# Two parts of one edit: the order of work behind the experts, and a norm's token factor behind its products

## What is computed

```python
# end of the first block
x = x + g2 * moe_ffn(h2, ...)          # each token: sum over 4 experts of weight * row, plus bias
x = rmsnorm(x, final_norm_w)
# the second block
h = concatenate([meta, x])             # 16 + 512 tokens
proj = rmsnorm_2(h, norm1_g) @ w_in    # queries first
...
h = h + mix @ w_out
hn = rmsnorm_2(h, norm2_g)             # h * rsqrt(mean(h*h) + eps) * g
gu = hn @ w_ffn_in                     # 1024 -> 2 * 2816
g, u = gu[..., :D_FF_2], gu[..., D_FF_2:]
h = h + (silu(g) * u) @ w_ffn_out
```

## Time and profile before

| | us |
|---|---|
| median of 3 runs | 3364.83 (3363.39 to 3370.04) |
| the profiled execution, its own time | 3360.08 |
| its span (first to last instruction) | 3358.2 |
| TensorE busy | 3205.9 (95%) |
| VectorE busy | 1330.0 (40%) |
| ScalarE busy | 725.3 (22%) |
| GpSimd busy | 400.2 (12%) |
| TensorE's share of the chain that ended last | 80% |
| VectorE's busy tenths in the slices of `ffn_in` | 2 to 4, mostly 3 |

### The profile page before, as it was taken

The page is one execution under the profiler, slowest core; times in us unless marked ns, Lnnn a source line. Parts: engine busy times, 40 slices in busy tenths (PEclk is TensorE's granted clock), DMA queues, the critical chain, the costliest instruction groups (busy, mean ns, idle before and its releaser), DMA issues.

```text
span 3358.2 us, 40420 instructions
## 1 busy us (share of the span) xinstructions
PE 3205.9 (95%) x13876; PEld 1897.5 (57%) x13877; DVE 1330.0 (40%) x2096; ACT 725.3 (22%) x1293; POOL 400.2 (12%) x312
## 2 busy tenths in 40 slices
PE   7999999999999999999999999999899999999999
PEld 5555555556488743333333333333587888788887
DVE  2544545455434532122122121221567577443342
ACT  3212121212021111111111111111224355211100
POOL 0222212132100100000000000000301254000000
PEclk9999999999999999999999999999899999999999
DMA  4211212124622369999999998888312121222111
GB/s 201 64 69 52 79 48 83 41 96 167 219 76 76 134 257 373 379 396 391 382 391 385 394 389 315 322 331 314 143 51 104 41 85 48 85 76 88 63 76 53
DMA packets 185079, 615.70 MB, mean 183 GB/s; under 512 B 18177, under 2 KB 55169, under 8 KB 174241
## 3 DMA queue, kind: packets, MB, share of 16 engines
q1 hardware_dynamic: 161216, 552.79, 43.1%
q0 software_dynamic: 10944, 39.85, 3.3%
q10 hardware_dynamic: 12832, 21.88, 1.8%
HBM read 578.01 MB, written 36.44 MB: 183 GB/s over the span
## 4 chain that ended last, share of the span: by engine, by line
PE 80%; DMA 5%; issue 5%; DVE 4%; POOL 2%; ACT 2%; SPq 1%; ACTq 0%; DVEq 0%; POOLq 0%
PE ps L322 24%; PE ps L2244 16%; PE ps L2218 11%; PE ps L1926 6%; PE ps L271 6%; DMA slot<-in_w_exp 5%; PE ps L1995 3%; PE ps L2467 2%; PE ps L2005 1%; PE ps L1971 1%; PE ps L1863 1%; PE ps L2439 1%; PE ps L2213 1%; PE ps L2422 1%; PE ps L2010 1%
## 5 line engine op out<-in xcount | busy, mean ns | idle before, releaser
L2244 PE MATMUL ps<-slot,xT_blk 128*64 128x512 f32 x3200 | 734.1, 599 | 26.4 <-DMA slot<-in_w_exp 23.8
L2244 PEld LDWEIGHTS ps<-slot,xT_blk 128*64 128x64 f32 x3200 | 218.0, 137 | 463.1 <-issue 376.1
L2218 PE MATMUL ps<-slot,aT 128*64 128x512 f32 x1632 | 361.1, 595 | 0.9 <-ACT aT L1634 0.9
L1926 PE MATMUL ps<-hT,slot 128*128 128x512 f32 (+1 forms) x896 | 308.9, 503 | 1.1 <-ACT small L1431 1.1
L2218 PEld LDWEIGHTS ps<-slot,aT 128*64 128x64 f32 x1632 | 116.9, 137 | 237.2 <-issue 237.2
L1926 PEld LDWEIGHTS ps<-hT,slot 128*128 128x128 f32 x896 | 168.9, 191 | 130.1 <-issue 121.1
L2966 DVE TENSOR_TENSOR gate<-ps,b_row 128x512 f32<-128x512 f32 x50 | 34.6, 692 | 517.8 <-PE ps L2244 517.6
L2587 DVE SCALAR_TENSOR_TENSOR conv<-ps,g_conv,conv 128x510 f32<-128x510 f32 (+1 forms) x224 | 133.3, 631 | 198.0 <-ACT conv L1444 194.6
L2962 DVE MEMSET b_there<- 128x1 f32 x50 | 3.0, 59 | 385.0 <-DMA b_few<-in_b_gu 376.4
L322 PE MATMUL ps<-in_t,in_s 128*128 128x264 f32 x528 | 124.8, 386 | 0.5 <-issue 0.5
L3334 POOL TENSOR_TENSOR token_there<-cst 128x1 f32<-128x1 f32 x25 | 4.9, 194 | 949.7 <-PE ps L2209 949.7
(11 more groups left out here) (501 smaller groups left out, 4769.8 us busy)
## 6 DMA issues: line engine op xcount, KB each, us to landing
slot<-in_w_exp SPq DMA_DIRECT2D x768, 512.0 KB, 8.5
in_w<-in_w_ffn SPq DMA_DIRECT2D x22, 1024.0 KB, 4.8
expert_rows<-zero SPq DMA_DIRECT2D x4, 4608.0 KB, 22.6
slot<-in_w_xbc SPq DMA_DIRECT2D x8, 2048.0 KB, 9.9
w_modT<-in_w_modT POOLq DMA_DIRECT2D x32, 512.0 KB, 3.5
rnn_w<-in_w_rnn SPq DMA_DIRECT2D x16, 1024.0 KB, 4.8
expert_rows<-y_row ACTq DMA_DIRECT2D x102, 128.0 KB, 5.6
out_w<-in_w_ffn_out SPq DMA_DIRECT2D x8, 1408.0 KB, 8.8
```

The lines of the kernel that those rows point to most:

```text
L1926: last = pe.matmul(ps[:, 2 * (m % 2) + part, 0:n], w[:, (k * 4 + m % 4) * P:(k * 4 + m % 4 + 1) * P], hT[:, k, c0:c0 + n], start=(k == 0), ...
L2218: last = pe.matmul(ps[h * UNIT:(h + 1) * UNIT, 6, :], aT[:, t, d * UNIT:(d + 1) * UNIT], slot[4 + d][:, t * D + h * 512:t * D + (h + 1) * ...
L2244: last = pe.matmul(ps[h * UNIT:(h + 1) * UNIT, 2 * s + t, :], xT_blk[:, k, s * UNIT:(s + 1) * UNIT], slot[i // 4][:, at:at + 512], start=( ...
```

## The change

Behind the experts:
- The filler ahead is 10 products instead of 19. `turn_sum` is split into `turn_last` (pick 3) and `turn_sum` (the identity over VectorE's sum). TensorE starts with block 0; the meta sum comes behind `turn_last(1)` and goes to bank 7. Each block's square sum moves to right behind the next block's turning.
- VectorE does picks 0, block 0 and picks 1 ahead of the meta steps; `invert(0)` and `invert(1)` come behind `add_picks(3)`, `add_back(2)` ahead of it.
- ScalarE takes a one-column square root ahead of the first pick, so that its table is there; the meta root comes behind the first block's square.
- GpSimd's `acc` waits for VectorE's last scaling (`scaled3_7`) instead of for the last square.

Second feed-forward:
- `Norm` is not used. ScalarE scales each tile of `h2nd` by the norm's weight straight into `xnT` and squares it; VectorE adds the squares tile by tile between the evictions of w_out; TensorE sums the result with 4 products, behind p1 and p2 of tile 0.
- The factor 1/root is multiplied on VectorE onto the four results of each tile (`by_root`: gate0, gate1, up0, up1), 88 multiplications of 128x264.
- The weight sums of tile 0 and `t1` are made between evictions; `in_s` and `in_t` change places in memory, and `root_m` moves.

```diff
-        keep_warm(19, 7)
-        back_act.after(pe, "meta_square")
-        for k in range(KD):
-            last = pe.matmul(ps[:, 6, 0:N_META], ones, square_meta[:, k, :], start=(k == 0), stop=(k == KD - 1))
-        back_pe.done(last, "meta")
+        keep_warm(10, 7)
...
+        turn_last(0)
         turn_sum(0)
+        turn_last(1)
+        back_act.after(pe, "meta_square")
+        for k in range(KD):
+            last = pe.matmul(ps[:, 7, 0:N_META], ones, square_meta[:, k, :], start=(k == 0), stop=(k == KD - 1))
+        back_pe.done(last, "meta")
         turn_sum(1)
         sum_squares(0)
+        turn_last(2)
         turn_sum(2)
+        sum_squares(1)
+        turn_last(3)
         turn_sum(3)
-        sum_squares(1)
         sum_squares(2)
         sum_squares(3)
```

```diff
+        back_dve.after(dve, f"bias{KD - 1}")
+        add_picks(0)
+        add_back(0)
+        add_picks(1)
         back_act.after(dve, "meta_root")
...
-        back_dve.after(dve, f"bias{KD - 1}")
-        add_picks(0)
-        add_back(0)
-        add_picks(1)
         add_picks(2)
         add_back(1)
+        add_back(2)
+        add_picks(3)
         invert(0)
-        add_picks(3)
-        add_back(2)
+        invert(1)
         add_back(3)
-        invert(1)
         invert(2)
```

```diff
+        act.activation(inverse_meta[:, 0:1], eps_col, ACT.Sqrt)
         first_pick(0)
+        first_pick(1)
+        squared(0)
         back_pe.after(act, "meta")
...
         first_pick(2)
-        squared(0)
         weighed(0)
         rooted(0)
         first_pick(3)
         squared(1)
         weighed(1)
+        rooted(1)
...
-        back_act.after(pool, f"square{TT - 1}")
+        back_dve.after(pool, f"scaled3_{KD - 1}")
```

```diff
-        norm2_2.on_act(act)
+        for j in range(KD):
+            out2.ev.after(act, f"tile{j}")
+            row2_act.done(act.activation(xnT[:, j, :], h2nd[:, j, :], ACT.Copy,
+                                         scale=prm[:, PRM["norm2_2"].start + j:PRM["norm2_2"].start + j + 1]), f"weighed{j}")
+            if j >= 3:
+                row2_dve.after(act, f"add{j - 2}")
+            row2_act.done(act.activation((square_m[j % 2] if j else square_sum)[:], h2nd[:, j, :], ACT.Square), f"square{j}")
...
-        norm2_2.on_pe(pe)
+        row2_act.after(pe, f"weighed{KD2 - 1}")
+        ffn_in.p1(pe, 0, in_ready(0))
         out2.ev.all(pe)
-        norm2_2.dve.after(pe, f"scaled{KD2 - 1}")
-        ffn_in.p1(pe, 0, in_ready(0))
-        norm2_2.dve.all(pe)
+        row2_act.after(pe, f"weighed{KD - 1}")
         ffn_in.p2(pe, 0)
+        row2_dve.after(pe, f"add{KD - 2}")
+        row2_act.after(pe, f"square{KD - 1}")
+        for l in range(2):
+            cols = slice(l * H2, (l + 1) * H2)
+            pe.matmul(ps[:, 5 + l, 0:H2], ones, square_sum[:, cols], start=True, stop=False)
+            last = pe.matmul(ps[:, 5 + l, 0:H2], ones, square_m[(KD - 1) % 2][:, cols], start=False, stop=True)
+        row2_pe.done(last, "sum")
         ffn_in.p1(pe, 1, in_ready(1))
```

```diff
+        def by_root(name, i, t, l):
+            ffn_in.dve.done(dve.tensor_tensor(t, t, root_m[:, l * H2:(l + 1) * H2], ALU.mult), f"{name}_{i}")
...
         in_done11(0)
+        for l in range(2):
+            cols = root_m[:, l * H2:(l + 1) * H2]
+            row2_act.after(dve, f"root{l}")
+            row2_dve.done(dve.reciprocal(cols, cols), f"inverse{l}")
+        row2_dve.all(dve)
+        ffn_in.dve.after(dve, "done11_0")
+        by_root("gate0", 0, ffn_gate[0][:, 0, :], 0)
```

More of the change, by code:

```diff
@@ L1209, in program @@
     out2 = Dense("out2", io["w_out2"], [0, 1], 1, 4, KD, H_PARTS, lambda k, p: attnT[:, k, p * H2:(p + 1) * H2], k_m(KD, 4), **second)
[L1210 to L1212 removed]
+    row2_act = Steps(sem("row2_act"), [n for j in range(KD) for n in (f"weighed{j}", f"square{j}")] + ["root0", "root1"])
+    row2_dve = Steps(sem("row2_dve"), [f"add{j}" for j in range(1, KD - 1)] + ["inverse0", "inverse1"])
+    row2_pe = Steps(sem("row2_pe"), ["sum"])
     FFN = KF
@@ L1832, in _ @@
         in_first11(0)
-        ffn_in.dve.after(act, "done11_0")
+        row2_pe.after(act, "sum")
+        for l in range(2):
+            row2_act.done(act.activation(root_m[:, l * H2:(l + 1) * H2], ps[:, 5 + l, 0:H2], ACT.Sqrt, scale=1.0 / D, bias=eps_col), f"root{l}")
+        ffn_in.dve.after(act, "gate0_0")
         ffn_in.act.done(in_silu(0, 0), "silu0_0")
```

109 lines of the change are left out of this document (62 added, 47 removed).

## The result

| | before | changed |
|---|---|---|
| median in the first comparison | 3364.11 us (4 runs, 3360.78 to 3370.04) | 3343.13 us (4 runs, 3338.86 to 3345.11) |
| ratio, 95% interval | | 0.9934 [0.9922, 0.9947] |
| median in a second comparison, in the last batch of runs | 3365.72 us (9 runs, 3361.99 to 3370.42) | 3339.39 us (4 runs, 3336.16 to 3342.15) |
| ratio, 95% interval | | 0.9915 [0.9900, 0.9930] |
| the profiled execution, its own time and span | 3360.08, 3358.2 us | 3344.28, 3342.5 us |

The changed kernel is faster by 21.0 us in one comparison and by 26.3 in the other, where 27.9 were forecast.

What follows compares the result with a forecast made beforehand. TensorE was taken to bound most of the span. 12.9 us after the experts plus 15.4 at the feed-forward less 0.45 gave 27.9 us; from 3360.08 to 3332.2, plus 4.75 to the median: 3337.0 us, range 3332 to 3346.

Steps and rivals of the forecast that it cites:

- What bounds the kernel, and the two places: Whole kernel: TensorE bounds most of the span; gains lie in the stage after the experts and the second feed-forward.
- Part two, 15.4 us: Entry of the second feed-forward: p7 of tile 0 starts at 2931.7 against 2947.12, 15.4 us earlier.
- tie: Feed-forward entry: ScalarE's silu and two copies end at 2931.6, level with TensorE; lateness 0 to 1.5 us, taken as 0.
- The loop, and +0.45 at its end: Second feed-forward's loop: four factor products per tile cost nothing inside it and 0.45 us at its end, up to 1.5.
- 3.2 us of room, 0.45 used: Feed-forward loop: the next weight sum is done 3.2 us before its p5; the fourth factor product uses 0.45.
- Adding back block 3 untouched by GpSimd (0 of 4.7): Stage after the experts: two GpSimd scalings over VectorE's adding back cost between 0 and 4.7 us, taken as 0.
- Block 2's scaling at 1.2: Stage after the experts: VectorE's scaling of block 2 takes 1.2 us without GpSimd beside it, seen at 2.60 before.
- GpSimd's additions behind the last scaling, 1.7 us: End of that stage: eight scalings at 0.34 us, so the first query tile takes 7.1 us instead of 8.8.
- The first query product 11.2 us earlier: Stage after the experts: the new order starts the query projection at 2413.5 instead of 2424.74.
- the first rival: Stage after the experts: low clock or late rows take part one's gain, 8 us lost, total 3345; chance 0.12.
- part one: Stage after the experts: 11.2 us from the new order plus 1.7 at the query tile, 12.9 us; range 7.5 to 14.
- The filler: Behind the bias products: 20 warm-up records instead of 38, six at the low clock, ending at 2382.6.

Runs made afterwards that it cites:

- three dead products: Changed kernel with three unused extra multiplications beside each factor product, 264 in all; 3334.42 us in one execution.
- part one alone: Kernel before with only the edit to the stage behind the experts, second feed-forward as before; 3355.45 us, ratio 0.9967 to the kernel before.
- again: The changed kernel run once more, word for word; 3339.39 us, ratio 0.9915 to the kernel before.
- two with dead products: Changed kernel with one or three unused multiplications beside each factor product; 3340.56 us with one, 3334.42 with three, one execution each.
- 19 fillers: Changed kernel with 19 filler products behind the bias instead of 10; 3344.19 us in one execution.
- block 3 drawn forward: Changed kernel plus five filler products behind the meta sum, with block 3's picks, turning and adding back moved earlier; 3339.24 us, ratio 0.9916 to the kernel before.
- filler and squares early: Changed kernel plus five filler products behind the meta sum, GpSimd's additions again waiting for the last square; 3335.05 us in one execution.

## Why the prediction was right, and where its sum was off

The forecast of 3337.0 us lies 6.1 us below the first median and 2.4 below the second, both inside its range. Point by point:

- **What bounds the kernel, and the two places**: right. The two edits move their own stretches and leave the 478.5 us between them alone.
- **Part two, 15.4 us**: right, 15.28, and so were its steps. The last eviction at 0.70, sums of 1.26 and 1.25, roots ready 0.5 behind the sums, reciprocals 3.46, gate factor 0.43. The factor is on the gate 9.9 us behind the last w_out record, and 9.8 were forecast. Its "tie" of ScalarE and TensorE was one: a chain 1.04 us later costs 0.76, so there is some 0.3 to spare.
- **The loop, and +0.45 at its end**: right, +0.46 (411.10 to 411.56). "3.2 us of room, 0.45 used" understated the room, since three of the four products fall into waits for TensorE; twelve more products of 0.35 start to start, 4.2 us a tile, still cost nothing in the loop.
- **Adding back block 3 untouched by GpSimd (0 of 4.7)**: right, 2.16 us beside 4.67 of GpSimd. Block 2's scaling at 1.2: right, 1.23.
- **GpSimd's additions behind the last scaling, 1.7 us**: mis-sized. From the first query product to the rotary sum it fell from 16.9 to 14.3, 2.6 us, of which 2.0 are shown to be this wait. The rule that was quoted from the Trainium skill (GPSIMD Engine Reference, Key points) held in the runs where it could be tried: with two inputs in SBUF a scaling has 0.34 alone and 1.01 on average with GpSimd beside it, and with one input in PSUM 0.34 both times.
- **The first query product 11.2 us earlier**: this is the step that failed in the profile of the changed kernel. Counted from the first bias product (2364.43 before) the table sets the forecast beside that profile and beside the run with three dead products, whose code up to here is the same:

| step | predicted | changed | three dead products |
|---|---|---|---|
| block 0 turned, VectorE starts on it | 22.1 | 23.67 | 22.23 |
| additions 1 done | 26.9 | 28.3 | 26.9 |
| block 2 turned | 34.7 | 38.4 | 35.8 |
| block 3 added back | 43.7 | 47.4 | 44.8 |
| first query product | 49.1 | 52.76 | 50.08 |
| first rotary sum | 64.3 | 67.08 | 64.39 |

Two things are missing from the forecast. The clock: "the new order's longest gap is 1.4 us" was said against the first rival; the gap was 1.3 to 1.4 in the five other runs without filler there and 2.7 or 2.8 in two, and the lower clock behind it cost 1.0 us in the last column and some 2 in the middle one. The first rival had the right mechanism at a fraction of its price of 8 us. The other is a start: VectorE began on block 0 1.5 us behind the end of TensorE's last record of the turning in the changed kernel (23.67, record over at 22.19), and so in part one alone; in every other run with this order it was 0.03 to 0.12. It was not VectorE that was slow: the chain above, which goes by the signals between engines, has TensorE's step end at 2397.23 (3.24 us from 2393.99, and 16 records take 1.95), 0.02 ahead of VectorE's start. So TensorE's signal came late, and the profile does not say why. Both differ between executions of the same code: over the five executions with this code (changed, again, part one alone, two with dead products) the stage has 67.08, 64.44, 66.97, 65.89 and 64.39, a mean of 65.8. That is 11.4 us less than the two executions with the old order (77.19, 77.13), where 12.9 was forecast. The best two of the five reach the forecast, but by two errors that cancel: their first query product comes 1.0 us later than forecast (50.1 instead of 49.1), and the tile behind it is 0.9 shorter (14.3 instead of 15.2).
- **What part one is made of** is shown for two of its terms only: some 2.5 us for the shorter filler (one execution) and 2.0 for GpSimd's additions. The other 7 or so, an estimate by what is left of the 11.4, are the new order itself with the collision that it removes; no run takes it apart.
- **The filler** was forecast to end 5.6 us behind the bias and took 7.1 in the first profile, 6.1 to 7.2 in all with ten products, with the lower clock over up to 5.2 us of it. The stage had 1 us of room for it, since VectorE's sum of block 0 comes only shortly before the last picks are turned.
- **The profiled execution against the median**: the forecast took its sum from an execution with the shortest experts' stage of the 14, and added the 4.75 us by which its time lay below the median. That was right, and also why the two profiles alone (3360.08 and 3344.28) show only 15.8 us.

By stretches the change is worth 11.4 + 15.3 - 0.5 = 26.2 us on average, against 27.9 forecast. The medians say 21.0 and 26.3. The experts' stage, which moves by more than the error of the sum, can make the difference between these.

What stays open: why TensorE's signal came 1.5 us late twice; why the same wait lowered the clock in five executions and not in two; how much of part one each move of the order gives; and whether the earlier order of block 3 is faster over all, which four or five executions a side can't tell.

## What to carry to other kernels

Cost an edit against the stretch that it changes and compare stretches between two fixed instructions, since a stage fed by transfers elsewhere can move by more than the edit is worth (here 9 us against 25). A factor that commutes with a product belongs behind it if its engine has room there, and dead copies of the added instruction measure that room cheaply. Where one engine's work lengthens that of the engine on the path, as GpSimd's did here (0.34 us to 1.01), what nobody waits for should start when the path is through. And a stage with waits like those here (1.3 to 2.8 us) should be budgeted at either clock, not at the better one.

## What the runs showed of the hardware that was not expected

- **The same wait, either clock.** Waits of 1.28 and 1.29 us ahead of the same 16 records, in the same code, were followed by a clock of 1.00 once and of about 0.5 in three (3.45 to 3.79 us for 16 records instead of 2.05 in the runs with dead products, 3.38 with 19 fillers). What lay ahead differed too: in the two executions that kept the clock without filler there, and in one with it, the bias products took 14.0 us and the 20 records of warm-up behind them 6.1 to 6.2; in those that lost it the bias products took 11.5 to 12.2 and the warm-up 6.5 to 7.2 (10.9 with 38 records). The granted clock was at 0.50 from the first bias product on in the former, and from 2.4 to 3.1 us behind it on in the latter. So the steps of the clock lie differently against the program in each execution. The Trainium skill (TensorE: Matmul & The Clock Gate, What's actually happening) says of the warm-up at a kernel's start that the number of matmuls at the lower clock varies from run to run of one kernel; the traces here show such a spread for later steps, up (16.0 to 17.2 us behind the first bias product in these executions) and down.
- **GpSimd and VectorE took turns.** A 128x128 scaling with two SBUF inputs: 0.34 us alone, 1.01 beside GpSimd's additions in two runs, 1.16 before (means of eight). One on 128x1024: 1.23 alone, 2.05 and 2.60 beside a scaling on GpSimd, and an addition of rows 1.28 alone and 3.47. With an input in PSUM: 0.34 both ways. It is no slowing in proportion: VectorE's instruction ended a fixed time behind the one that GpSimd had running, whatever their overlap. For 128x1024 it was 1.08 behind 2409.62 (start 2407.23, 3.47 long) and 2422.14 in the kernel before, and 1.09 behind 2417.85 with block 3 drawn forward (start 2416.89, 2.05 long); for 128x128 it was 0.15 (2417.34 and 2417.49, 2418.69 and 2418.83 with filler and squares early). GpSimd waited likewise: an addition begun at 2412.46 beside a scaling on VectorE that ended at 2413.50 took 2.16 instead of 1.27.
- **One late transfer.** The first weights of the output matrix were late by 1.0 to 1.5 us in most runs, by 3.0 in the changed kernel again and by 2.9 with block 3 drawn forward. In the first of these two the clock was down behind it, and 22 records took 8.15 us instead of 5.16.
- **An identical stage that varies by 8.6 us** (1162.5 to 1171.1), with 69 to 77 waits for the experts' weights of together 23.8 to 28.3 us, and the stretch ahead of it by 6.7 (1198.7 to 1205.4).
